# Moving modulation units of the first MLP from TensorE to VectorE in 512-column tiles, with all raw weight units split in halves

## The reference, cut to what matters

```
def adaln(cond, w, b):
    m = jax.nn.silu(cond) @ w + b
    m = m.reshape(cond.shape[0], 6, 1, D_MODEL)
    return [m[:, j] for j in range(6)]

def modulate(x, g, shift, scale):
    return rmsnorm(x, g) * (1 + scale) + shift

def sq_relu_mlp(h, w1, w2):
    return jnp.square(jax.nn.relu(h @ w1)) @ w2

for l in range(DEPTH):
    sh1p, sc1p, g1p, sh2p, sc2p, g2p = adaln(c_ctx[None], w_ada[l], b_ada[l])
    sh1s, sc1s, g1s, sh2s, sc2s, g2s = adaln(c, w_ada[l], b_ada[l])
    ...
    xp = xp + g1p * rmsnorm(yp, norm_g[l, 1])
    mp = sq_relu_mlp(modulate(xp, norm_g[l, 2], sh2p, sc2p), w1_mlp[l], w2_mlp[l])
    xp = xp + g2p * rmsnorm(mp, norm_g[l, 3])
```

## Time and profile before

| what | us |
|---|---|
| median of 3 runs | 2494.47 |
| range of the runs | 2492.38 to 2500.18 |
| profiled execution, its own time | 2498.91 |
| its span, first to last instruction | 2497.1 |
| PE busy | 2440.8 (98%) |
| DVE busy | 1668.2 (67%) |
| ACT busy | 1069.0 (43%) |
| POOL busy | 265.0 (11%) |
| DMA | 651.35 MB, 261 GB/s on average |

### The profile page before, as it was taken

The page is one execution under the profiler, slowest core; times in us unless marked ns, Lnnn a source line. Parts: engine busy times, 40 slices in busy tenths (PEclk is TensorE's granted clock), DMA queues, the critical chain, the costliest instruction groups (busy, mean ns, idle before and its releaser), DMA issues.

```text
span 2497.1 us, 36507 instructions
## 1 busy us (share of the span) xinstructions
PE 2440.8 (98%) x13794; PEld 1994.0 (80%) x13794; DVE 1668.2 (67%) x1902; ACT 1069.0 (43%) x1279; POOL 265.0 (11%) x465
## 2 busy tenths in 40 slices
PE   6899999999999999999999999999999999999998
PEld 3578888778888888888887877798888888888887
DVE  2246666586777777775568877665788688564665
ACT  3234433463433433333364356575534334343343
POOL 0021111000110110000012144200001001000000
PEclk8999999999999999999999999999999999999999
DMA  9989999968987987988877856659568668665565
GB/s 360 367 279 337 322 321 298 321 221 269 339 285 254 325 284 252 326 268 261 292 250 249 293 185 216 223 191 293 186 221 293 201 220 280 206 199 194 179 208 164
DMA packets 454341, 651.35 MB, mean 261 GB/s; under 512 B 18264, under 2 KB 312984, under 8 KB 452568
## 3 DMA queue, kind: packets, MB, share of 16 engines
q1 hardware_dynamic: 422560, 543.45, 65.6%
q0 software_dynamic: 29312, 105.12, 12.4%
q10 hardware_dynamic: 2360, 1.32, 0.2%
HBM read 634.39 MB, written 15.43 MB: 260 GB/s over the span
## 4 chain that ended last, share of the span: by engine, by line
PE 82%; DMA 6%; DVE 5%; ACT 4%; issue 2%; SPq 0%; ACTq 0%; DVEq 0%
PE PS L1382 19%; PE PS L1463 14%; PE PS L1464 13%; PE PS L1465 13%; PE PS L1385 10%; PE PS L1411 3%; DMA RAW<-in_w_mlp 3%; DVE WLO L1997 2%; ACT WHI L1708 2%; DMA SCR<-in_w_ada 1%; DMA RAW<-in_w_o_na 1%; PE PS L1601 1%; PE PS L1602 1%; PE PS L1603 1%; PE PS L1576 1%
## 5 line engine op out<-in xcount | busy, mean ns | idle before, releaser
L1997 DVE TENSOR_TENSOR WLO<-RAW,WHI 128x2048 fp32r<-128x2048 f32 x228 | 519.5, 2295 | 298.5 <-ACT WHI L1708 298.1
L1382 PE MATMUL PS<-HM,WHI 128*128 128x512 f32 x2560 | 648.5, 395 | 2.2 <-issue 1.8
L1382 PEld LDWEIGHTS PS<-HM,WHI 128*128 128x128 f32 x2560 | 459.5, 189 | 101.2 <-issue 17.0
L1708 ACT ACTIVATE WHI<-RAW 128x2048 fp32r<-128x2048 f32 x228 | 431.3, 1910 | 216.9 <-DMA RAW<-in_w_mlp 142.5
L1463 PE MATMUL PS<-WHI,HID 128*128 128x512 f32 x1152 | 450.6, 391 | 2.1 <-DVE WLO L1997 2.1
L1464 PE MATMUL PS<-WLO,HID 128*128 128x512 f32 x1152 | 448.4, 389 | 0.0
L1465 PE MATMUL PS<-WHI,HID 128*128 128x512 f32 x1152 | 448.2, 389 | 0.0
L1385 PEld LDWEIGHTS PS<-HM,WLO 128*128 128x128 f32 x2560 | 348.3, 190 | 28.5 <-DVE WLO L1997 3.5
L1385 PE MATMUL PS<-HM,WLO 128*128 128x256 f32 x2560 | 357.1, 282 | 0.8 <-DVE WLO L1997 0.8
L2073 DVE SCALAR_TENSOR_TENSOR X<-X,CS 128x1024 f32<-128x1024 f32 x240 | 297.0, 1279 | 1.2
L1718 ACT ACTIVATE WHI<-RAW 128x1024 fp32r<-128x1024 f32 x154 | 163.3, 1060 | 306.6 <-DMA RAW<-in_w_mlp 158.0
(11 more groups left out here) (261 smaller groups left out, 2204.3 us busy)
## 6 DMA issues: line engine op xcount, KB each, us to landing
RAW<-in_w_mlp SPq DMA_DIRECT2D x144, 1024.0 KB, 6.2
ADW<-in_w_ada SPq DMA_DIRECT2D x114, 1024.0 KB, 10.1
RAW<-in_w_mlp SPq DMA_DIRECT2D x224, 512.0 KB, 6.0
X<-in_w_ada POOLq DMA_DIRECT2D x224, 256.0 KB, 4.2
RAW<-in_w_qkv_na SPq DMA_DIRECT2D x46, 1024.0 KB, 8.2
RAW<-in_w_qkvg_gla SPq DMA_DIRECT2D x60, 512.0 KB, 5.3
RAW<-in_w_qkvg_gla SPq DMA_DIRECT2D x18, 1024.0 KB, 5.9
SCR<-in_w_ada SPq DMA_DIRECT2D x16, 1024.0 KB, 11.5
```

Source lines behind the costliest of these rows:

```text
L1382: return mm(bank[:, 0:2 * T2], hi[:, k, P * b:P * b + P], act[:, kc, 0:2 * T2], start=first, stop=False)
L1708: actv(WHI[:, 2 * s + u, 0:n], RAW[:, u, 0:n], ACT.Copy).then_inc(hi_done, 1)
L1997: tt(WLO[:, 2 * s + u, 0:n], RAW[:, u, 0:n], WHI[:, 2 * s + u, 0:n].bitcast(f32), ALU.subtract).then_inc(lo_done, 1)
```

## The change

**Fewer units on PE.** In the first MLP, PE makes four units in a group (the two in the out slabs are gone). The stage of the first output projection (WO0) makes one more, the second one (WO1) two fewer. The records of line 1411 go from 1568 to 1280, nine units of 32.

**More units on DVE, in smaller tiles.** In groups 0 to 2 of the first MLP, DVE makes six units ("block"): 48 tiles of 128 rows by 512 columns, each one DMA of 256 KB by GpSimd. Two tile buffers (`STILE`) of 512 columns take the place of two of 1024, because the six accumulators fill the rest of `X`. Group 3, which had none, makes four units in 32 tiles. `UP_SHARE` puts 3 (in group 3: 2) tiles in each up slab but the first, `OUT_SHARE` puts 7, 7, 7, 6 (in group 3: 9, 9, 0, 0) in the out slabs. PE adds them up with `block_rows`: in groups 0 to 2 after the last out slab's quarter 3, in group 3 after quarter 1 of out slab 2; each waits for all tiles of its group. ACT stores six (four) rows in `block_store`, before the first out slab of the next group (in group 3 in the last out slab). `X` comes back only after group 3's rows, and ACT's squares of x0 and x1 move into the last out slab.

**Squares.** In the first MLP ACT makes the ReLU and then the square (`square_hidden`, four instructions of 128x256 for a slab), where DVE had made both in two.

**Halves.** Every raw unit behind the start goes through in halves, each with its own DMA, rounding and subtraction, and the first half is loaded again once its own subtraction is done.

The core of the diff:

```diff
-        PU = NB + 2
-        GU = PU + QU
+        PU, SIX = NB, 6
+        GU = PU + SIX
...
-        PLAN_WO0, PLAN_WO, PLAN_V = ((0,), (1,), (), ()), ((0,), (1,), (), ()), ((), (), (), ())
-        PLAN_MLP = ((0,), (1,), (), ())
+        PLAN_WO0 = ((0,), (1,), (2,), ())
+        PLAN_WO = PLAN_V = PLAN_MLP = ((), (), (), ())
...
+        SACC = {c: [XF[:, 1024 + YC * c * b:1024 + YC * c * (b + 1)] for b in range(2)] for c in (2, 3)}
+        STILE = [XF[:, YC * q:YC * (q + 1)] for q in range(2)]
+        UP_SHARE, OUT_SHARE = {3: (3, 3, 3, 3, 3, 3, 3), 2: (2, 2, 2, 2, 2, 2, 2)}, {3: (7, 7, 7, 6), 2: (9, 9, 0, 0)}
...
             def load_slab(m, w, row, col, after=1):
                 for u in range(2):
+                    sp.wait_ge(lo_half if after == 1 else lo_done, (m - after) * 2 + u + 3)
+                    sp.dma_start(dst[:, 0:UKC // 2, :], src[:, 0:UKC // 2, :]).then_inc(raw_half[u], 16)
                     sp.wait_ge(lo_done, (m - after) * 2 + u + 3)
-                    sp.dma_start(RAW[:, u, :].rearrange("p (c n) -> p c n", c=UKC), src).then_inc(raw_in[u], 16)
+                    sp.dma_start(dst[:, UKC // 2:UKC, :], src[:, UKC // 2:UKC, :]).then_inc(raw_in[u], 16)
...
+            def block_rows(q, pairs):
+                pe.wait_ge(block_step, q * BLOCK_TILES + KC * pairs)
+                pe.wait_ge(block_row, q + 1)
+                pe.wait_ge(pick_ready, 2 * 2)
...
+                    if pairs == 3 and n == YN - 1 and x == 3:
+                        block_rows(g, pairs)
+                    if pairs == 2 and n == 2 and x == 1:
+                        pe.wait_ge(mod_done, 3)
+                        block_rows(g, pairs)
...
+            def block_store(q, pairs, unit):
+                act.wait_ge(block_summed, q + 2)
+                act.wait_ge(block_out, q * (16 * SIX) + 16)
+                copy = actv(SROW[:, 0:UC], ROWS_TB[:, 0:UC], ACT.Copy)
+                if pairs == 3:
+                    copy = actv(SROW[0:64, UC:2 * UC], ROWS_TB[0:64, UC:2 * UC], ACT.Copy)
+                copy.then_inc(block_row, 1)
+                act.wait_ge(block_row, q + 2)
+                for j in range(2 * pairs):
+                    row = SROW[32 * (j % 4):32 * (j % 4) + 8, UC * (j // 4):UC * (j // 4) + UC]
+                    act.dma_start(mod_rows[ds(unit + j, 1)].rearrange("o h b j n -> (o b j) h n"),
+                                  row.rearrange("p (h n) -> p h n", h=2)).then_inc(block_out, 16)
...
             def fetch_rows(i):
+                if blocks:
+                    act.wait_ge(block_out, 16 * sum(2 * p for p in BLOCK_PAIRS[:blocks]) + 16)
...
+            def square_hidden(k, slab):
+                for b in range(2):
+                    act.wait_ge(bank_free, slab * 2 + b + 5)
+                    actv(RELU[:, b, :], RELU[:, b, :], ACT.Relu).then_inc(relu_done, 1)
+                for b in range(2):
+                    act.wait_ge(relu_done, k + b + 1)
+                    actv(RELU[:, b, :], RELU[:, b, :], ACT.Square).then_inc(square_done, 1)
...
+            def block_tile(q, pairs, t):
+                k, c, slot = t // pairs, t % pairs, t % 2
+                dve.wait_ge(block_in[slot], q * (8 * BLOCK_TILES) + (16 * (t // 2) + 16))
...
+                        end = nc.vector.scalar_tensor_tensor(acc, STILE[slot], CS[:, k, b:b + 1], acc, ALU.mult, ALU.add)
+                end.then_inc(block_step, 1)
...
-            def out_slab(m0, n, stage, add, f=None, last=False, quad=None):
+            def out_slab(m0, n, add, f=None, last=False, quad=None, tiles=None, share=0):
                 m = m0 + 2 * n
-                split_lo_halves(m + 1, 1, stage * 14 + 4 * n)
+                split_lo(m + 1, 1, (0,))
+                if share > 4:
+                    tiles(1)
+                split_lo(m + 1, 1, (1,))
+                if share > 4:
+                    tiles(1)
...
+                split_lo(m + 2, 0, (0,))
+                if share > 4:
+                    tiles(1)
+                split_lo(m + 2, 0, (1,))
+                if share > 4:
+                    tiles(share - 3)
...
+            def block_load(q, t):
+                pairs = BLOCK_PAIRS[q]
+                if q or t >= 2:
+                    pool.wait_ge(block_step, q * BLOCK_TILES + (t - 1))
+                pool.dma_start(STILE[t % 2], w_ada[unit // edge, P * k:P * k + P, unit % edge * UC:unit % edge * UC + YC]) \
+                    .then_inc(block_in[t % 2], 16)
```

More of the change, by code:

```diff
@@ L14 @@
 from contextlib import ExitStack
+import itertools
 import numpy as np
@@ L908, in gla_scalar @@
                 if n == 0:
+                    act.wait_ge(block_out, 16 * sum(2 * p for p in BLOCK_PAIRS) + 16)
                     quad_store(QV, QUAD_UNITS[QV], QUADS_VB, QROW_V)
@@ L1820, in out_slab @@
                     return
-                if n < YN - 1:
-                    split_hi_halves(m + 2, 0, stage * 14 + (4 * n + 2))
-                elif not last:
-                    split_hi(m + 2, 0, UNIT, range(2), keys)
-                for a, at in () if early else ada:
+                if not last:
+                    split_hi(m + 2, 0, range(2), keys)
+                for a, at in ada:
                     ada_row(a)
                     store_row(a, at)
-                if 0 < n < YN - 1:
+                if 0 < n < YN - 1 and f != 1:
                     more_squares(f, (("x0",), ("x1",))[n - 1])
@@ L1954, in mlp_group @@
                         slab = g * (4 * NB) + i * 2 + (m + s)
-                        ada = (g * PU + i + a, g * GU + i + (a + SKIP0)) if s == 1 and a is not None else None
-                        step(slab, s, ada, (g * KC + i * 4 + (layer * HID_GROUPS * KC + 2 * s), i, s))
-                if quad is not None:
-                    quad_store(*quad)
+                        ada = (g * PU + i + a, g * GU + i + (a + SKIP0 + block)) if s == 1 and a is not None else None
+                        step(slab, s, ada, (g * KC + i * 4 + (layer * HID_GROUPS * KC + 2 * s), i, s), True, bool(block))
+                if store is not None:
+                    store()
                 m0 = g * (4 * NB) + (m + 2 * NB)
@@ L2074, in quad_tile, with tiles_of, run @@
                 end.then_inc(quad_step, 1)
+            def block_tile(q, pairs, t):
+                k, c, slot = t // pairs, t % pairs, t % 2
+                dve.wait_ge(block_in[slot], q * (8 * BLOCK_TILES) + (16 * (t // 2) + 16))
+                if k == 0 and c == 0:
+                    dve.wait_ge(block_summed, q + 1)
+                if k:
+                    dve.wait_ge(block_step, q * BLOCK_TILES + (t - pairs + 1))
+                for b in range(2):
+                    acc = SACC[pairs][b][:, YC * c:YC * c + YC]
+                    if k:
+                        end = nc.vector.scalar_tensor_tensor(acc, STILE[slot], CS[:, k, b:b + 1], acc, ALU.mult, ALU.add)
+                    else:
+                        end = ts(acc, STILE[slot], CS[:, k, b:b + 1], None, ALU.mult)
+                end.then_inc(block_step, 1)
+            def tiles_of(q, pairs):
+                number = iter(range(KC * pairs))
+                def run(count):
+                    for t in itertools.islice(number, count):
+                        block_tile(q, pairs, t)
+                return run
             def quad_out_tile(q, n, x):
@@ L2339, in mlp_group, with hidden_body @@
                 for n in range(YN):
-                    out_slab(g * (4 * NB) + (m + 2 * NB), n, g + (H_MLP0, H_MLP1)[layer], add, 2 * layer + 1 if complete else None,
-                             complete and layer and n == YN - 1, quad=quad)
-            def hidden_body(g, i, layer, m, quad=None, tiles=()):
+                    out_slab(g * (4 * NB) + (m + 2 * NB), n, add, 2 * layer + 1 if complete else None,
+                             complete and layer and n == YN - 1, quad, tiles, OUT_SHARE[pairs][n] if pairs else 0)
+            def hidden_body(g, i, layer, m, quad=None, tiles=(), run=None, shares=(0, 0)):
                 for s in range(2):
```

326 lines of the change are left out of this document (177 added, 149 removed).

## The result

The changed kernel takes **2581.14 us** (median of 5 runs, 2580.13 to 2583.95), the kernel before 2496.07 (5 runs beside them). The ratio is 1.034, 95% interval 1.0329 to 1.0351: slower by 3.4%, on the side that was forecast (2520), but beyond the top of the range, 2549. The profiled execution is 2580.13, its span 2578.0 against 2497.1.

What follows compares the result with a forecast made beforehand. PE, busy 98% of the span, was taken as the bound. Savings of 16.8 and 2.5 us against 37.9 of waits, 5.1 of clock, 0.9 and 1.3 gave +25.9 us: forecast 2520 us, range 2485 to 2549.

Steps and rivals of the forecast that it cites:

- the tile's round trip: DVE's out slabs: with two buffers, 4.0 us from a tile read to its buffer's next use; slab 22.9 against PE's 22.0.
- DVE keeps up: Rival, chance 0.16: tile waits fall where DVE would wait for block_done anyway, nothing is late, 2477 us.
- short landings: Rival, chance 0.12: single 256 KB loads land faster than traced pairs, round trip about 3.0 us, total 2496, no change.
- the reckoning of how late DVE's queue is at the end of an out part: Groups 1 and 2: last tile done 96.7 us after PE's start, PE ready at 88.0, so it waits 8.7 us.
- DVE's first split starts at 7.3: Out part of groups 1 and 2: DVE begins 7.3 us after PE's start, after ACT copies and stores the rows.
- the up slabs fall behind too: Rival, chance 0.07: landings of 5.9 make DVE's up slab 12.6 of 12.2, out part entered 3 us later; 2550 or more.
- Its splits are late by less, so nothing adds: Out parts of groups 1 and 2: late DVE splits add no PE wait beyond the 8.7 us before block_rows.
- As the new out slabs have none: Out slabs: no ADW loads beside the tile loads, so a landing was taken as 3.6 us.
- Group 3, 14.6: Group 3's out part: PE wants quarter 2's split of slab 2 at 55.0, DVE has it at 69.6; 14.6 us wait.
- The clock, 5.1: Behind PE's waits of 6 to 9 us: slow granted clock costs 1.7 us three times, 5.1 in all.
- Two of them and the eight matmuls of the quad (about 0.5 us): PE's out part before the change: two units at 1.86 us each plus about 0.5 us of matmuls, leaving 88.1 for four slabs.
- L = 3.7: Low case for a tile buffer's time between uses, 3.7 instead of 4.0 us: 2504 us without clock loss.

Runs made afterwards that it cites:

- tiles at hand: Changed kernel, DVE computing again and again on two tiles already there while loads go unread; rerun without a fault of the first try (2648.71 us): 2511.3 us, ratio 1.0068.
- e12: Changed kernel with third buffer, later selection, new tile places, late X return, ACT's stores in the up part, PE's groups 1 and 2 written out: 2493.59 us.

## Why the prediction was right in direction and wrong in size

**Right.** The mechanism: the tile's round trip, carried in DVE's queue to PE. POOL's reaction was 0.3 (a tile done at 1157.32, the next load issued at 1157.61), a landing 4.1 in the median, and DVE's tile waits in a middle out slab of group 2 were 0.8 and 2.2, the 3 us that were forecast. With the tiles at hand, 56.8 of the 64.5 us of excess in groups 0 to 2 went. The squares cost nothing, as said; the halves gave 4.5 where the sum had 1.6. The rivals "DVE keeps up" and "short landings" were false: the shortest landing of all tiles was 2.8. The estimate by the Trainium skill's "DMA: Bandwidth & Descriptors", section "Anatomy of one DMA", 2.6 us, lies below that too.

**Wrong.** The sum said +25.9, the trace has +80.9. Of the missing 55.0, 33.6 is idle time (37.6 in the sum, 71.2 measured), 17.7 clock (5.1 and 22.8) and 3.7 the longer selections. The step that failed first is the reckoning of how late DVE's queue is at the end of an out part. In group 2 the last tile was to be done 96.7 us after PE's start; it was done after 111.1. Of these 14.4 us, 5.4 are the later start, 4.1 the three slabs behind it (73.7 instead of 69.6) and 4.9 the last slab. PE's waits at the three selections were 10.3, 8.9 and 11.4, where 5.9, 8.7 and 8.7 were forecast, and PE itself had come there late, by waits that the sum had at nothing.

*"DVE's first split starts at 7.3."* In group 2 it started at 12.65. DVE came late out of the up part, because its tiles there waited too (3.47 and 1.13 us in the rows above): the rival "the up slabs fall behind too", with a chance of 0.07, held in part. And the copies and six stores of ACT took 4 us in front of its first rounding. The run with the tiles at hand divides the two: it has the same stores, and there the first split of group 2 starts at 8.8 (PE's out part starts at 1025.98):

```profile
1034.81 2.36 DVE L2057 TENSOR_TENSOR WLO<-RAW,WHI 128x1024 fp32r<-128x1024 f32 x2 [4.50 <-ACT WHI L1740]
```

So some 3.8 us of the delay are the up part's tile waits and 1.5 are ACT's. PE's wait at this place was 4.00 in the changed kernel and 0.18 in that run.

*"Its splits are late by less, so nothing adds."* Ten waits for splits in groups 0 to 2 add 19.6 us to the 30.6 at the selections: 50.2, where I had 23.3. The prediction had named waits at the splits as a sign of being wrong. No evacuation of DVE's waited for PE inside these out parts. What held DVE up there were tiles that had not landed (17.5, 19.0 and 17.9 us in groups 0, 1 and 2) and ACT's roundings (3.4, 7.4 and 7.9).

*"As the new out slabs have none"* (no `ADW` load). True for three slabs; in the last one SP is ahead of the engines and loads for the next group. The last tile took 8.3 us from issue to use (1157.61 to 1165.90) instead of 4, and the slab 24.7 us instead of 19.9. That the `ADW` loads are the cause is read from the order of the issues, in three groups alike; no run took them away.

*Group 3, 14.6.* It was 24.4: 9.6 for the gain, 8.2 for the selection, 6.6 for splits. I had followed DVE's tiles, but not what stands behind them in its queue (the gain PE turns in slab 1), nor POOL's queue, in which a store, a wait for its landing and four loads stand ahead of tile loads. Moving that chain alone gave nothing, though: the wait for the gain shrank and the one for the selection grew.

*The clock, 5.1.* I priced three of the four long waits, at 1.7 each. There were 18 in the first MLP, and the granted clock was 0.93 to 0.95 over whole out parts and 0.83 over the late part of the last. That this time is a consequence of the waits is shown by the versions without them: with 5.5 us of waits for splits and none at the selections (e12), the clock of the execution is 0.994 again, as before the change, and PE is busy for 2428.3 us with the same 13546 instructions, 22.2 less.

*"Two of them and the eight matmuls of the quad (about 0.5 us)."* The trace has 16 records there, 1.07 us. The sum has no term for the selections that take their place, 3.7 us more in all. With it the units save 13.1 and not 16.8; the repaired version's PE is busy for 12.5 us less than before.

A slip of the range: by the sum's own weights, L = 3.7 without loss of clock gives 2507, not 2504.

Open: the last group took 210.8 us in the best version, 11 above its own work (202.4 before, two units fewer, a selection more). The waits that its trace lists are 8.8 us, of which 3 were there before; what the rest consists of is not known. A version that takes `X`'s squares off ACT's last slab wasn't tried.

## What to carry to other kernels

Count the buffers of a streamed operand for the place where most of its uses follow each other without other work between them, with the landing time of the busiest stretch. Here the third buffer gave 41 us, new places without it nothing, and with it another 16 (2517.7 to 2501.5); freeing the engine of other work gave nothing either. Let an engine that isn't late wait for one that is only where that one has had time to catch up: moving the selection by one slab gave 34 us alone, and 23 on top of the third buffer (together with the gain's chain, which alone gave nothing), without making anything faster. When work is taken from the engine that is the bound, count every queue that gets some of it, in-order waits included, and add PE's clock to the waits: nine units of 1.87 us saved were no gain in any version here over the 2491 us that the halves alone gave.

## What was not expected of the hardware

A 256 KB load took 2.8 us at the least and 4.1 in the median, but 6.9 to 8.2 when issued just behind two 1 MB loads, and 10.3 and 10.7, the longest, just behind four gain loads. A 512 KB half issued right behind the 2 MB of `X` and those gain loads took 15.6. And the 18 waits of 0.2 to 11 us, 75 us in all, cost another 22 in clock: three tenths on top, 1.2 us a wait, where I had 1.7 from the one stage end. The price is uneven. Behind the waits of 0.56 and 1.09 us (groups 0 and 1) the granted clock of the next 2 us reads 1.00. Behind the one of 2.20 (group 0) it is 0.50 for 2 us, and behind the one of 10.31 it is 0.50, the level of 1.2 GHz, for 5 us.
